# Moving projection matmuls inside the levels of a triangular inverse, in a two-block fp32 kernel on one core

## The reference, cut to what matters

```
beta = sigmoid(b);  G = cumsum(g) within a chunk
lower = strict_tril(beta * (k k^T) * decay)
[u, w] = solve(lower + I, [v * beta, k * beta * exp(G)])     # unit lower triangular
for each chunk n:
    v_new = u_n - w_n S
    o_n   = (q exp(G)) S + ((q k^T) * decay) v_new
    S     = S * exp(G_last) + k_gained^T v_new
```

## Time and profile before

| | us |
|---|---|
| median of 3 runs | 2456.33 (2454.56 to 2460.14) |
| the profiled execution | 2460.14 |
| its span, first to last instruction | 2458.4 |
| PE busy | 2262.8 (92%) |
| DVE busy | 1225.6 (50%) |
| ACT busy | 995.0 (40%) |
| POOL busy | 795.9 (32%) |
| mean granted TensorE clock | 0.957 of full speed |

### The profile page before, as it was taken

How to read it: one execution, slowest core, us unless ns; L and a number is a source line. 1 busy time by engine, 2 the same in 40 slices (tenths; PEclk the granted TensorE clock), 3 DMA queues, 4 the chain that set the end, 5 groups by cost and what they waited for, 6 DMA issues and landing times.

```text
span 2458.4 us, 31847 instructions
## 1 busy us (share of the span) xinstructions
PE 2262.8 (92%) x10614; PEld 1799.1 (73%) x10614; DVE 1225.6 (50%) x1917; ACT 995.0 (40%) x1630; POOL 795.9 (32%) x352
## 2 busy tenths in 40 slices
PE   3899999998699999969979999999899989999997
PEld 2687777776578888748847888888766657888886
DVE  6366766644433332279964333326466764333322
ACT  4433444433444432265544444223255554444322
POOL 2522222222444444420014444446100103444442
PEclk8999999999799999979989999999699989999998
DMA  3211110112222232201102222322000001222221
GB/s 123 94 35 43 34 43 34 42 35 73 73 77 94 99 104 97 87 29 54 49 28 86 94 102 94 141 101 86 18 18 17 17 9 69 94 96 101 100 102 72
DMA packets 43690, 169.96 MB, mean 69 GB/s; under 512 B 4848, under 2 KB 4976, under 8 KB 43120
## 3 DMA queue, kind: packets, MB, share of 16 engines
q1 hardware_dynamic: 43056, 163.82, 19.2%
q10 hardware_dynamic: 576, 5.37, 0.5%
HBM read 167.08 MB, written 2.10 MB: 69 GB/s over the span
## 4 chain that ended last, share of the span: by engine, by line
PE 79%; DVE 9%; issue 5%; ACT 4%; POOL 1%; DVEq 1%; DMA 0%; ACTq 0%; POOLq 0%; SPq 0%
PE bank L282 21%; PE bank L284 20%; PE bank L283 20%; PE bank L1727 2%; PE bank L699 2%; PE bank L707 2%; PE bank L712 1%; DVE ACC L382 1%; PE bank L1520 1%; ACT Pr L1778 1%; PE bank L1709 1%; POOL WL L247 1%; PE bank L1279 1%; PE bank L1280 1%; PE bank L1278 1%
## 5 line engine op out<-in xcount | busy, mean ns | idle before, releaser
L247 POOL TENSOR_TENSOR WL<-raw,WR 128x1024 fp32r<-128x1024 f32 (+2 forms) x274 | 707.3, 2581 | 1002.6 <-ACT WR L243 997.9
L282 PE MATMUL bank<-XR,WR 128*128 128x512 f32 x1528 | 625.8, 410 | 52.6 <-DVE XL L403 31.8
L284 PE MATMUL bank<-XR,WL 128*128 128x512 f32 x1528 | 602.4, 394 | 0.0
L283 PE MATMUL bank<-XL,WR 128*128 128x512 f32 x1528 | 602.1, 394 | 0.0
L243 ACT ACTIVATE WR<-raw 128x1024 fp32r<-128x1024 f32 (+2 forms) x230 | 256.2, 1114 | 733.9 <-PE bank L284 726.7
L282 PEld LDWEIGHTS bank<-XR,WR 128*128 128x128 f32 x1528 | 290.9, 190 | 131.5 <-issue 35.8
L282 PE MATMUL bank<-MR,WR 128*128 128x512 f32 (+1 forms) x856 | 338.2, 395 | 16.1 <-DVE ML L1444 7.9
L284 PEld LDWEIGHTS bank<-XR,WL 128*128 128x128 f32 x1528 | 290.9, 190 | 62.6
L283 PEld LDWEIGHTS bank<-XL,WR 128*128 128x128 f32 x1528 | 291.8, 191 | 60.9 <-issue 6.4
L283 PE MATMUL bank<-ML,WR 128*128 128x512 f32 (+1 forms) x856 | 334.0, 390 | 0.0
L284 PE MATMUL bank<-MR,WL 128*128 128x512 f32 (+1 forms) x856 | 333.8, 390 | 0.0
(11 more groups left out here) (285 smaller groups left out, 2819.2 us busy)
## 6 DMA issues: line engine op xcount, KB each, us to landing
raw<-w SPq DMA_DIRECT2D x224, 512.0 KB, 3.2
raw<-w SPq DMA_DIRECT2D x48, 704.0 KB, 4.0
raw<-w SPq DMA_DIRECT2D x16, 384.0 KB, 3.0
hT<-xT SPq DMA_DIRECT2D x1, 2048.0 KB, 8.2
hT<-xT ACTq DMA_DIRECT2D x1, 2048.0 KB, 8.1
phi<-phi ACTq DMA_DIRECT2D x1, 2048.0 KB, 10.2
out<-Y SPq DMA_DIRECT2D x8, 256.0 KB, 2.0
memT<-memT ACTq DMA_DIRECT2D x1, 1024.0 KB, 8.0
```

What stands on the lines that cost most here:

```text
L247: nc.gpsimd.tensor_tensor(WL[:, here], raw[:, here], WR[:, here].bitcast(F32), ALU.subtract).then_inc(weight_split, 1)
L282: nc.tensor.matmul(into, wr, xr(k0 + k), start=start, stop=False)
L283: nc.tensor.matmul(into, wr, xl(k0 + k), start=False, stop=False)
L284: mm = nc.tensor.matmul(into, wl, xr(k0 + k), start=False, stop=stop)
```

## The change

In levels 0 to 4 there were three chunks between A and U, and none between T and the next A. Now there is one between A and U and two behind T. Level 5 has one between A and U, as before, and two behind U, as before (these were taken after the loop over the levels, and are now taken in it). No instruction is added or removed, and the number of chunks up to each level is the same.

```diff
@@ in head_tensor, the loop over levels
                 mm.then_inc(s_["A_done"], 1)
-                gap(3 if lv < LEVELS - 2 else 1)
+                gap(1)
                 pe.wait_ge(s_["A_ready"], h * 6 + (lv + 1))
...
                     mm.then_inc(s_["T_done"], 1)
-            gap(2)
+                gap(2)
             pe.wait_ge(s_["pT_ready"], h + 1)
```

## The result

The median went from 2456.27 to 2473.55 us (ratio of the runs 1.0069, 95% interval 1.0047 to 1.0091). The forecast was 2460.8, with a range up to 2468: the sign was that of the sum, the size nearly four times it (17.3 against 4.5). The profiled execution of the changed kernel took 2471.77 us, with a span of 2470.0, 11.6 more than that of before. From the first head's query product to the last head's the changed kernel took 15.0 us more in these two traces; the rest was 3.4 shorter, and nothing in the change gives a reason for that.

The account below looks back on a forecast made before the run. TensorE's own order was taken as the bound; +0.56 levels, +0.10 ScalarE, +0.03 VectorE and GpSimd made +0.69 a loop head, +4.1 for six, +0.4 outer heads: +4.5 us, 2460.8. Range 2456 to 2466, widened to 2455 to 2468.

Parts of the forecast that it names:

- What bounds the kernel, and the level: TensorE's own order bounds the kernel; a loop-head level goes from 4.97 to 5.10 us, gaining 0.20, losing 0.33.
- the waits cancel: Rival, chance 0.10: level 5's 0.33 wait is special, levels 0 to 4 cost 5.02 against 4.97, total 2458.3.
- faster: Rival, chance 0.10: one chunk hides ScalarE's copy at levels 0 to 4, 0.20 a level comes back, 2448.
- The sum for the two outer heads: First and last head: +0.16 us each for the levels, plus ScalarE's 0.10 in the first, together +0.4.
- ScalarE at level 5: After the last A, take(2) at +0.20, silu at +0.69, queue free about +1.2; cost 0.10 us in seven heads.
- VectorE and GpSimd in level 2: Line 914 starts inside line 247 and ends 0.55 after it; some 0.15 us of cover left, cost 0.
- VectorE and GpSimd in levels 4 and 5: Line 776 freed, unit 2's split later under a tap; v_new 3.96 to 4.25 us after U, cost +0.03.
- In level 4 line 776 is freed: VectorE's tap at level 4 is no longer held, so level 5's U would be taken after 1.20 instead of 1.30.
- Cost -0.1 to +0.2, I take +0.03: Per loop head, the forecast change in v_new's delay behind level 5's U, 4.07 us before.
- VectorE becomes late: Rival, chance 0.18: holds at line 914 and the tap after level 5's U, 0.5 to 0.8 us a head, 2464 to 2467.
- its two signs: U's subtraction starting later than 1.2 us after its product; v_new more than 4.3 us after U.
- No case of its own: TensorE's clock, fallen to half once in these heads: one fall more or less moves the time by less than 2 us.

Follow-up runs that it names:

- e1: Against the kernel before: levels 0 to 3 have one chunk before U and two behind T, level 4 keeps three and none; 2458.38 us, ratio 1.0003.
- e2: Against the kernel before: only level 4 is changed, to one chunk before U and two behind T; 2472.17 us, ratio 1.0056.
- e3: Kernel before with one chunk before U in every level; behind T two in levels 0 to 2, four in 3, none in 4; 2460.76 us, ratio 1.0011.
- e6: Changed kernel, but in the heads' units GpSimd makes the low part (line 247) for 128 of 1024 columns only; 2458.41 us, ratio 1.0011.
- e7: Changed kernel with VectorE's two third-row taps of level 4 moved from ahead of level 5's U to behind it; 2479.52 us, ratio 1.0092.
- e8: Kernel before with two chunks before U, one behind T in levels 0 to 3, and line 854 moved behind the first copy of S; 2443.50 us, ratio 0.9945.
- e10: e8 with the last two third-row taps moved from ahead of the first v_new to behind the second; 2441.65 us, ratio 0.9930 to the kernel before.

## Why the prediction was wrong

**What bounds the kernel, and the level.** Right, and with it the rivals "the waits cancel" and "faster" are out for the loop heads. 0.20 lost for VectorE's U, 0.33 for ScalarE's copy, a new level of 5.10: measured 5.10. Level 0 without the second wait has 0.93 instead of 1.01 from chunk to U in the loop heads, as the 0.08 was read. The first A to the last U was to grow by 0.66 with ScalarE's 0.10; measured 0.63. The sum for the two outer heads has a slip: it takes 0.08 off for six levels, but level 5's is in the kernel before as well, so it should be 0.64 - 0.40 = 0.24 and not 0.16. Measured were 0.17 in the first and 0.20 in the last. Over the first seven heads the levels cost 4.0 us, and that is nearly all of the 4.5 forecast.

**ScalarE at level 5.** Right: take at + 0.20, silu at + 0.69, the copy at 326.08, + 1.21, where + 1.10 would have been free.

**VectorE and GpSimd in level 2.** Right, narrowly. VectorE in level 2 to 3 after the change:

```profile
314.09 1.47 DVE L914 TENSOR_TENSOR low_a<-lower,table 128x512 f32<-128x512 f32 x1
...
317.69 0.69 DVE L908 TENSOR_TENSOR U<-U,bank 128x512 f32<-128x512 f32 x1 [0.23 <-PE bank L707]
```

Line 914 is held, as forecast, and 0.23 of cover is left where 0.15 was worked out.

**VectorE and GpSimd in levels 4 and 5.** This is the step that failed: "In level 4 line 776 is freed" and "Cost -0.1 to +0.2, I take +0.03". Line 776 was not freed but waited 1.45 us for take(2), and v_new came 1.31 us a head later behind U's product, +9.2 in all. The prediction followed one consequence of the later 24th chunk, ScalarE's take(2), to the copy of A behind it, and not to the tap that waits for take(2) (line 764), two queues on. With that wait in the sum the rest could have been worked out from the rows: 247 ends 3.9 us behind the last A instead of 1.9, the first tap can't start before A + 0.8, where take(2) ends (its 0.20 and 0.60; measured A + 0.94), so the second runs into 247, and line 904 ended 0.55 after 247 in the earlier trace rows: that gives about A + 4.4, measured 329.30 - 324.87 = 4.43. e1, e2 and e3 show that the place of the 24th chunk is the cause, e6 that GpSimd's hold is needed for it. That the tap's wait is needed too is worked out and was not tried alone: VectorE was done with T at 324.36, and without the wait both taps (0.48 and 0.75 when nothing holds them) would have ended before 247 began at 326.32.

**The rivals.** The third, "VectorE becomes late", names the right engine and the right kind of hold, and its two signs came (U's subtraction 2.62 us after its product, v_new 5.38). But it put the hold on line 914 in level 2 and on the tap behind level 5's U, and priced it at 0.5 to 0.8 us, 2467 at most. It was the tap ahead of U, which was not in view, and it cost 1.31.

**The clock.** "No case of its own" was too easy. In the first seven heads of the changed kernel's trace the clock fell within 2.2 us behind v_new three times, in e2 once and in e7, which has the one long wait, five times. In the nine traces without these waits it never fell there. So the waits give the falls a place that they did not have. How many it adds is open: the falls 12 us behind v_new come and go without these waits (none to two in a trace), and each kernel has one trace. It is +1.8 us in this pair, and 11.5 to 22.4 us is what the interval of the ratio leaves for the total. What share of the median's 17 us is the clock stays open: the heads explain 15.0 in the traces.

## What to carry to other kernels

- When an instruction moves, list every queue that its end releases, and then what waits in turn for those: here one chunk set off a copy on ScalarE, a split on GpSimd and, through the copy, a tap on VectorE, and two of them collided.
- A gap on TensorE is best shared by what each wait needs: two chunks covered the copy, one covered the subtraction, and three and none or one and two each missed one of them.
- Moving work from one side of a wait to the other gives nothing where that engine's queue is the bound up to the next handover (e7); taking the work out of that stretch does (e8; e10 by its trace, as the times of e8 and e10 overlap).

## What was not expected of the hardware

- A 128x512 VectorE operation with its tensors in SBUF that started while GpSimd's line 247 ran ended a fixed time after it: with two tensors read 0.55 us after (2.63 us for a 0.75 us tap, 1.47 for a 0.68 us product), with one (line 776) 0.28 after (1.52 us for 0.48). The cast of line 227 does the same: line 776 took 0.71 beside it after the change. Level 2's subtraction of U, which reads PSUM, took 0.69 beside 247 in both kernels' traces. The Trainium skill, page SBUF — State Buffer, section "SBUF: two separate sides", calls this an exclusive lock; the traces agree, and e6 shows it by the length of 247.
- The granted clock fell to 0.50 of full right behind two waits of TensorE of about 0.90 and 1.11 us with one product and one chunk between them. The same two waits stand in all seven heads of the changed kernel, and it fell in three of them.
